# Copying 70 weight chunks inside device memory into contiguous rows before the expert stage

## The reference, cut to what matters

```
pl = modulate(xl, norm1, sh1_l, sc1_l) @ w_in          # 1024 x 6832, the last 4096 columns are gate logits
...                                                    # four mixers on parts of pl: MLA, GQA, mLSTM, Hyena
acc = sum_i sigmoid(gate_i) * (y_i @ w_branch[i])
x = x + g1 * (acc @ w_out)                             # 1024 x 1024
h = modulate(x, norm2, sh2, sc2)
q = h @ peer_wq                                        # 1024 x 2048, eight heads of 256 columns
...                                                    # scores against subkeys, top 16 of 16384 experts per head
out[t] = sum_k share * gelu(peer_u[idx[t,k]] . h[t]) * peer_v[idx[t,k]]
```

## Time and profile before

| | us |
|---|---|
| median of 3 runs | 3304.91 |
| lowest, highest | 3304.67, 3307.84 |
| the profiled execution, its own time | 3291.54 |
| span in its trace | 3289.6 |
| PE busy | 2295.7 |
| DVE busy | 1749.9 |
| POOL busy | 1740.7 |
| ACT busy | 692.3 |
| moved by DMA | 1028.54 MB |

### The profile page before, as it was taken

How to read it: one execution, slowest core, us unless ns; L and a number is a source line. 1 busy time by engine, 2 the same in 40 slices (tenths; PEclk the granted TensorE clock), 3 DMA queues, 4 the chain that set the end, 5 groups by cost and what they waited for, 6 DMA issues and landing times. The chain is left out here.

```text
span 3289.6 us, 32042 instructions
## 1 busy us (share of the span) xinstructions
PE 2295.7 (70%) x10877; PEld 1373.1 (42%) x10877; DVE 1749.9 (53%) x4736; ACT 692.3 (21%) x1336; POOL 1740.7 (53%) x1580
## 2 busy tenths in 40 slices
PE   5999998778957787566777587645799455434435
PEld 2776687644524555232553155321577322101001
DVE  1202335567685556666556745573234766666662
ACT  2235532134111120211102211110442111010000
POOL 0010000467675566777676677776000577777775
PEclk8999999888667898777897588765779767555555
DMA  7677223899999999999999999998302999999997
GB/s 283 209 269 245 64 65 99 293 356 381 323 377 339 354 393 385 350 369 370 374 388 377 342 364 397 398 377 348 115 7 84 311 407 402 404 393 394 405 384 309
DMA packets 395065, 1028.54 MB, mean 313 GB/s; under 512 B 31890, under 2 KB 176282, under 8 KB 393754
## 3 DMA queue, kind: packets, MB, share of 16 engines
q0 software_dynamic: 232064, 847.35, 67.2%
q1 hardware_dynamic: 162794, 179.15, 16.3%
q10 hardware_dynamic: 48, 0.01, 0.0%
HBM read 1019.05 MB, written 7.34 MB: 312 GB/s over the span
## 5 line engine op out<-in xcount | busy, mean ns | idle before, releaser
L1942 POOL DMA_INDIRECT expert_rows<-in_peer_u,chosen x768 | 884.8, 1152 | 840.6 <-DVE chosen L2298 583.2
L2190 DVE CUSTOM_DVE_ANT_0 expert_rows<-expert_rows,h_rows 128x1024 f32<-128x1024 f32 x768 | 937.0, 1223 | 601.0 <-DMA expert_rows<-in_peer_u,chosen 580.8
L2082 PE MATMUL ps<-expert_rows,weights 128*32 128x512 f32 x3072 | 594.0, 855 | 681.3 <-DMA expert_rows<-in_peer_v,row_of 679.3
L1955 POOL DMA_INDIRECT expert_rows<-in_peer_v,row_of x768 | 826.9, 1077 | 403.9 <-PE ps L2082 200.3
L2082 PEld LDWEIGHTS ps<-expert_rows,weights 128*32 128x32 f32 x3072 | 77.2, 125 | 963.5 <-issue 953.0
L1613 PE MATMUL ps<-front,arena 128*128 128x256 f32 x1536 | 384.0, 407 | 76.5 <-DMA arena<-in_w_in 75.7
L1613 PEld LDWEIGHTS ps<-front,arena 128*128 128x128 f32 x1536 | 308.2, 205 | 163.0 <-DMA arena<-in_w_in 59.1
L654 PE MATMUL ps<-front,arena 128*128 128x256 f32 (+1 forms) x816 | 200.0, 403 | 42.6 <-DMA arena<-in_w_in 39.2
L2010 PE MATMUL ps<-h,wq 128*128 128x256 f32 x768 | 200.9, 416 | 2.4 <-ACT h L443 2.4
L654 PEld LDWEIGHTS ps<-front,arena 128*128 128x128 f32 (+1 forms) x816 | 158.6, 198 | 87.9 <-DMA arena<-in_w_in 34.3
L2010 PEld LDWEIGHTS ps<-h,wq 128*128 128x128 f32 x768 | 156.6, 211 | 55.0 <-issue 30.0
(11 more groups left out here) (360 smaller groups left out, 3159.0 us busy)
## 6 DMA issues: line engine op xcount, KB each, us to landing
arena<-in_w_in SPq DMA_DIRECT2D x79, 1024.0 KB, 14.3
arena<-in_ada_w POOLq DMA_DIRECT2D x40, 1024.0 KB, 6.6
wq<-in_peer_wq SPq DMA_DIRECT2D x48, 512.0 KB, 9.4
arena<-in_w_out SPq DMA_DIRECT2D x12, 1024.0 KB, 7.8
expert_rows<-in_peer_u,chosen POOLq DMA_INDIRECT x768, 6.6
expert_rows<-in_peer_v,row_of POOLq DMA_INDIRECT x768, 6.7
ada_w<-in_ada_w SPq DMA_DIRECT2D x4, 2048.0 KB, 23.4
arena<-in_w_branch SPq DMA_DIRECT2D x16, 512.0 KB, 3.4
```

The costliest lines, as they stand in the source:

```text
L1942: nc.gpsimd.indirect_dma_start(x.ring[:, j % self.R, :], None, self.u_rows, bass.IndirectOffsetOnAxis(x.chosen[:, w, q:q + 1], 0)).then_in ...
L1955: nc.gpsimd.indirect_dma_start(x.ring[:, j % self.R, :], None, self.v_rows, bass.IndirectOffsetOnAxis(x.rows[:, w % 4, 4 * c + r:4 * c + r ...
L2082: ins = nc.tensor.matmul(m.ps[to:to + 32, half, :], flat[:, r * P + 32 * c:r * P + 32 * c + 32], x.ring[:, self.place_of["v", a] % self.R, ...
L2190: nc.vector.tensor_tensor_reduce(u, u, x.ht, 1.0, 0.0, ALU.mult, ALU.add, x.dots[:, at:at + 1]).then_inc(self.u_dotted, 1)
```

## The change

A new part, `Relay`, is put into the plan of `opening` behind the two parts that finish the modulation. In it GpSimd issues transfers from memory to memory, with three semaphores in turn, so that a new one is issued when the third before it has landed; its last tick waits for all. Each transfer takes one chunk of weights (runs of 1 KB) and writes it to a tensor of its own in which each of the 128 rows holds all that one partition gets: 8 KB for a chunk of 256 columns of `w_in` or `w_out`, 4 KB for a query chunk. The loads in `experts_beside` then read those tensors. The loads of `opening`, `closing` and `experts` stay as they were. `Projection` packs a chunk's columns without gaps in its ring place.

```diff
+class Relay(Part):
+    FLIGHT = 3
+    def __init__(self, sems, copies):
+        self.copies, self.ticks = copies, len(copies)
+        self.copied = sems(*[f"copied{j}" for j in range(self.FLIGHT)])
+
+    def gpsimd(self, pool, i):
+        to, src = self.copies[i]
+        if i >= self.FLIGHT:
+            pool.wait_ge(self.copied[i % self.FLIGHT], 16 * (i // self.FLIGHT))
+        pool.dma_start(to, src).then_inc(self.copied[i % self.FLIGHT], 16)
+        if i == self.ticks - 1:
+            for j in range(self.FLIGHT):
+                pool.wait_ge(self.copied[j], 16 * len(range(j, self.ticks, self.FLIGHT)))
...
-        sp.dma_start(self.ring[:, c % 2, :, 0:n], self.w_in[:, :, c0:c0 + n]).then_inc(self.ins[c % 2], 16)
+        weights = self.w_in[:, :, c0:c0 + n] if self.flat is None else self.flat[c0, n]
+        sp.dma_start(self.packed(c), weights).then_inc(self.ins[c % 2], 16)
...
-        plan += braid(whole(heads), g[:14], q[54:]) + [(rest0, 0), (rest1, 0)]
+        plan += braid(whole(heads), g[:14], q[54:]) + [(rest0, 0), (rest1, 0)] + whole(Relay(sems, m.copies))
         plan += braid(whole(attn), whole(conv), g[14:22])
...
+        gated = [(O_GATE + 256 * c, 256) for c in range(16)]
+        asked = [(0, 256), (O_GQA, 256), (O_ML, 256), (O_ML + 768, 256), (O_HY, 256), (O_HY + 256, 256), (O_HY + 512, 256)]
+        all_asked = [(0, 256), (256, 160), (O_GQA, 256), (O_GQA + 256, 256), (O_ML, 256), (O_ML + 256, 256), (O_ML + 512, 256),
+                     (O_ML + 768, 272), (O_HY, 256), (O_HY + 256, 256), (O_HY + 512, 256)]
+        for h in range(PH):
+            for c in range(2):
+                flat = nc.dram_tensor(f"flat_q{h}_{c}", (P, KD // 2 * T), F32, kind="Internal").ap()
+                m.flat_q[h, c] = flat.rearrange("p (k n) -> p k n", k=KD // 2)
+                m.copies.append((m.flat_q[h, c], d["peer_wq"][0].rearrange("(k p) n -> p k n", p=P)[
+                    :, 4 * c:4 * c + 4, h * T:(h + 1) * T]))
+        for flats, w, wanted in ((m.flat_in[0], d["w_in"][0], asked + gated), (m.flat_out, d["w_out"][0], [(256 * c, 256) for c in range(4)]),
+                               (m.flat_in[1], d["w_in"][1], all_asked + gated)):
+            for at, n in wanted:
+                flat = nc.dram_tensor(f"flat{NUMBER[1]}", (P, KD * n), F32, kind="Internal").ap()
+                flats[at, n] = flat.rearrange("p (k n) -> p k n", k=KD)
+                m.copies.append((flats[at, n], w.rearrange("(k p) n -> p k n", p=P)[:, :, at:at + n]))
```

More of the change, by code:

```diff
@@ L536, with __init__ @@
 class Projection(Part):
-    def __init__(self, nc, sems, m, w_in, bias, f, kv, s, own, keys, ring, gbias, banks, after, room=(), normed=None, h=None, ahead=False):
-        self.ahead = ahead
+    def __init__(self, nc, sems, m, w_in, bias, f, kv, s, own, keys, ring, gbias, banks, after, room=(), normed=None, h=None, ahead=False, flat=None):
+        self.ahead, self.flat = ahead, flat
         self.h = f.h if h is None else h
@@ L623, in load, with packed @@
         c0, n = self.chunks[c]
-        sp.dma_start(self.ring[:, c % 2, :, 0:n], self.w_in[:, :, c0:c0 + n]).then_inc(self.ins[c % 2], 16)
+        weights = self.w_in[:, :, c0:c0 + n] if self.flat is None else self.flat[c0, n]
+        sp.dma_start(self.packed(c), weights).then_inc(self.ins[c % 2], 16)
+    def packed(self, c):
+        n = self.chunks[c][1]
+        return self.ring[:, c % 2, :, :].rearrange("p k n -> p (k n)")[:, 0:KD * n].rearrange("p (k n) -> p k n", k=KD)
     def sync(self, sp, i):
@@ L649, in tensor @@
         for k in range(KD):
-            w = self.ring[:, c % 2, k, at:at + n]
+            w = self.packed(c)[:, k, at:at + n]
             if i == 0 and self.normed is not None:
@@ L1560, with __init__ @@
     ticks = len(STEPS) + 2
-    def __init__(self, nc, sems, m, w_in, f, ring, sig, banks, after, branches, room=None, flip=0, away=None):
-        self.away = away
+    def __init__(self, nc, sems, m, w_in, f, ring, sig, banks, after, branches, room=None, flip=0, away=None, flat=None):
+        self.away, self.flat = away, flat
         self.room_for, self.flip = room if room else [after, after], flip
@@ L1581, in load @@
         at = O_GATE + 256 * c
-        sp.dma_start(self.ring[:, (c + self.flip) % 2, :, 0:256], self.w[:, :, at:at + 256]).then_inc(self.ins[c % 2], 16)
+        weights = self.w[:, :, at:at + 256] if self.flat is None else self.flat[at, 256]
+        sp.dma_start(self.ring[:, (c + self.flip) % 2, :, 0:256], weights).then_inc(self.ins[c % 2], 16)
     def sync(self, sp, i):
@@ L1735, with __init__ @@
     ticks = KD + 1
-    def __init__(self, nc, sems, m, mod, w_out, acc, ring, lo, banks, after, room):
+    def __init__(self, nc, sems, m, mod, w_out, acc, ring, lo, banks, after, room, flat=None):
+        self.flat = flat
         self.nc, self.m, self.mod, self.acc, self.ring, self.lo, self.banks, self.after = (
@@ L1747, in load @@
             sp.wait_ge(self.mult, 2 * (c - 1))
-        sp.dma_start(self.ring[:, c % 2, :, 0:256], self.w[:, :, c * 256:(c + 1) * 256]).then_inc(self.ins[c % 2], 16)
+        weights = self.w[:, :, c * 256:(c + 1) * 256] if self.flat is None else self.flat[256 * c, 256]
+        sp.dma_start(self.ring[:, c % 2, :, 0:256], weights).then_inc(self.ins[c % 2], 16)
     def sync(self, sp, i):
@@ L1797, with __init__ @@
     R, LV = 10, 20
-    def __init__(self, nc, sems, m, mod, d, l, passes, h, x, banks, after, kept=1):
+    def __init__(self, nc, sems, m, mod, d, l, passes, h, x, banks, after, kept=1, flat=None):
+        self.flat = flat
         self.nc, self.m, self.mod, self.d, self.l, self.passes, self.h, self.x = nc, m, mod, d, l, passes, h, x
@@ L1889, in ask_queries @@
     def ask_queries(self, sp, b, c, head):
-        sp.dma_start(self.x.wq[:, b, c, :, :], self.d["peer_wq"][self.l].rearrange("(k p) n -> p k n", p=P)[
-            :, 4 * c:4 * c + 4, head * T:(head + 1) * T]).then_inc(self.wq_in[2 * b + c], 16)
+        weights = self.d["peer_wq"][self.l].rearrange("(k p) n -> p k n", p=P)[:, 4 * c:4 * c + 4, head * T:(head + 1) * T]
+        if self.flat is not None:
+            weights = self.flat[head, c]
+        sp.dma_start(self.x.wq[:, b, c, :, :], weights).then_inc(self.wq_in[2 * b + c], 16)
     def place(self, v):
@@ L2561, in experts_beside @@
         norm2l = Norm(nc, sems, m, mod, 3 * KD, CTX, h2, m.rs, 7, (), False, True)
-        peer = Peer(nc, sems, m, mod, d, l, [CTX, 0], h2, x, (2, 3), [])
-        proj = Projection(nc, sems, m, d["w_in"][l], bias(l), f, kv, 0, True, False, ring, gbias[:, :], (4, 5), [])
+        peer = Peer(nc, sems, m, mod, d, l, [CTX, 0], h2, x, (2, 3), [], flat=m.flat_q)
+        proj = Projection(nc, sems, m, d["w_in"][l], bias(l), f, kv, 0, True, False, ring, gbias[:, :], (4, 5), [],
+                          flat=m.flat_in[0])
         heads = Heads(nc, sems, m, vec, d, l, f, kv, 0, True, False, heads_memory(arena, Z), (6, 7),
@@ L2571, in experts_beside @@
         gates = Gates(nc, sems, m, d["w_in"][l], f, cut(arena, Z, 2, KD, 256), cut(arena, Z + 4096, 12, T), (4, 5),
-                      conv.done, branch)
+                      conv.done, branch, flat=m.flat_in[0])
         branch.gates = gates
@@ L2575, in experts_beside @@
                         [(branch.acc_done, len(STEPS)), (gates.mult, len(STEPS)), (gates.out, len(STEPS))],
-                        [(gates.mult, len(STEPS))])
+                        [(gates.mult, len(STEPS))], m.flat_out)
         norm2c = Norm(nc, sems, m, mod, 3 * KD, 0, h2, cut(arena, 2048, T), 6,
@@ L2589, in experts_beside @@
         proj_n = Projection(nc, sems, m, d["w_in"][l + 1], bias(l + 1), f, kv, 1, True, True, ring, gbias[:, :], (4, 5),
-                            known, known)
+                            known, known, flat=m.flat_in[1])
         heads_n = Heads(nc, sems, m, vec, d, l + 1, f, kv, 1, True, True, heads_memory(arena, Z), (6, 7), proj_n.done)
         gates_n = Gates(nc, sems, m, d["w_in"][l + 1], f, cut(arena, Z, 2, KD, 256), cut(arena, Z + 4096, 12, T), (4, 5),
-                        heads_n.done, None, away=sigs)
+                        heads_n.done, None, away=sigs, flat=m.flat_in[1])
         conv_n = Hyena(nc, sems, m, vec, d, f, hyena_memory(arena, 0, Z), spectra, (4, 5, 6),
@@ L2638, in build @@
         sigs = nc.dram_tensor("sigs", (P, len(STEPS), T), F32, kind="Internal").ap()
+        gated = [(O_GATE + 256 * c, 256) for c in range(16)]
+        m.flat_out, m.flat_in, m.copies = {}, [{}, {}], []
+        asked = [(0, 256), (O_GQA, 256), (O_ML, 256), (O_ML + 768, 256), (O_HY, 256), (O_HY + 256, 256), (O_HY + 512, 256)]
+        all_asked = [(0, 256), (256, 160), (O_GQA, 256), (O_GQA + 256, 256), (O_ML, 256), (O_ML + 256, 256), (O_ML + 512, 256),
+                     (O_ML + 768, 272), (O_HY, 256), (O_HY + 256, 256), (O_HY + 512, 256)]
+        m.flat_q = {}
+        for h in range(PH):
[7 more added lines that the diff above has]
+            for at, n in wanted:
```

(4 more changed lines are left out.)

## The result

The changed kernel takes 3252.19 us (median of 4 runs, 3247.76 to 3256.75) against 3306.38 us; the ratio is 0.9831, 95% interval [0.9807, 0.9854]: 54 us faster. In a later comparison of more runs it took 3241.52 us against 3303.61, ratio 0.9808 [0.9775, 0.9842]. The forecast had been slower by 72 us; what came is rival A, whose price was 44 us.

What follows compares the result with a forecast made beforehand. Opening bound by TensorE with DMA engines three quarters idle, expert stage bound by DMA; +126 (copy overrun) - 36 (loads) - 18 (waits) = +72 us, so 3364 profiled, 3377 on the median; range 3235 to 3435.

Steps and rivals of the forecast that it cites:

- rival A: Engines from 306 to 569 us: copies overlap read and write, no overrun, 44 us won, about 3261; chance 0.39.
- What bounds the kernel: Opening bound by TensorE with DMA engines three quarters idle; expert stage, 569 to 2295 us, bound by DMA.
- What a copy costs: Copies in the opening at 200 GB/s take 323 us, end at 695 us, 126 us after the old end.
- the low end: Copies in the opening: read and write side by side at the slower's 348 GB/s, 186 us, nothing added.
- the point that decided (258): Copy rate in GB/s at which the opening's overrun equals the expert stage's gain of 54 us.
- the forecast's own range: Whole kernel: 3305 + 105 - 60 = 3350 to 3305 + 175 - 45 = 3435 us.
- GpSimd's issuing: Opening: issuing 70 copies occupies GpSimd 50 to 201 us, inside 263 either way; nothing added.
- The opening's own loads: Opening's weight chunks, sharing engines with copies: 0 to 40 us on the PE path, nothing taken; about 10 if copies fit.
- The loads after it: Expert stage: 73.1 MB go from 1 KB runs to 8 KB (queries 4 KB), 210 to 174 us, 36 saved.
- Waits that go: Expert stage: chunks landing sooner release PE and ring slots sooner; 18 us taken, between 0 and 42.
- the check of the stage: Expert stage: rows at 395 and SP's loads at 348 GB/s give 1628 of 1726 us, explaining it up to 98.
- B: Expert stage: expert rows, not weights, set it, so 36 and 18 fall away; +126, 3431; chance 0.09.

Runs made afterwards that it cites:

- the 1 KB landings: The change with ring rows 272 columns apart, so a partition's 8 KB land in eight 1 KB pieces: 3305.44 us, ratio 1.0020 to the kernel before.

## Why the prediction was wrong

**What bounds the kernel**: right. The opening had its DMA engines three quarters idle, the expert stage is bound by them, and the stage shrank as bytes per microsecond rose.

**What a copy costs**: this step failed, and with it the sign. I took 200 GB/s, by the argument that "a copy passes it twice", reading and writing in turns, and priced 323 us of the engines and an overrun of 126 us. The runs show 347 to 354 GB/s, some 187 us, the low end of 186, and no overrun: the copies are done near 545 us, before 570, the sign that the prediction had named for this step. Reading and writing do not take turns, which by the 419 GB/s of the earlier trace rows would give 209 at most. The argument had nothing in the rows to rest on; that loads and stores each run at 419 GB/s alone (a level, not a bound: single slices of the earlier trace rows stand at 433 to 459) says what a single direction does, not what both do together, and the middle between two guesses of one kind was taken where the ends, 174 and 348, lay on either side of the point that decided (258). The reason given for the low end fell too: long source runs leave the rate where it is. Why it is 350 and not 419 stays open; it hangs on neither the length of the source's runs nor the number in flight (344 with two, while the queue's packets move); rows written other than 4 and 8 KB long were not tried.

The Trainium skill, page "DMA: Bandwidth & Descriptors", section "Latency and other measured facts", has 214 GB/s per direction for copies between memory tensors issued from the sync and scalar queues. This kernel's copies, with GpSimd as the issuer and rows of 4 and 8 KB, ran at 350; the measurement decides. The +105 in the forecast's own range is the overrun by that 214; by the 209 of the rows it would have been +113.

**GpSimd's issuing**: no part of the bound, as said; a copy of 1 MB occupies GpSimd 0.84 us, near the lower of the bounds (0.72 to 2.9).

**The opening's own loads**: nothing in the sum, "about 10 us" in rival A. Measured 18.1 us: a chunk takes 19.2 us to land where doubling gave 10. A share of one half was assumed between the two queues; what the runs show is that a queue with 1 KB packets gets little beside one with 3.8 KB (12.6 us with two copies in flight, 19 with three, 22.7 with six) and less beside 6.1 KB (33 us, three in flight).

**The loads after it**: 36 us by 73.1 MB at 348 and 419 GB/s. SP's queue took 274 us of the engines before and 240 after, 34 less: this term was right in size and reason, and the 1 KB landings confirm it from the other side (265).

**Waits that go**: 18, out of 0 to 42. The stage lost 69; 34 are SP's packets, and 18 are the expert rows' own packets, 1389 us of the engines in place of 1407. That leaves 17 for time in which neither queue's packets moved, so this term came out near its size.

**The other queue's packets**: nothing in the sum, measured 18. Short packets also cost the long ones beside them: in the five profiles whose w_in chunks all move in 1 KB packets, short landings among them, the expert rows' packets take 1404 to 1410 us of the engines, in the others 1388 to 1394. The earlier trace rows had room for it: 81.5% of 1726 us is 1407, where 395 GB/s gives 1359. That is half of the 98 us that the check of the stage left unexplained, and I passed over it.

**Rivals**: A came, at 54 us (62 in the later comparison) where 44 was its price, with 34 + 18 + 17 - 18 = 51 in the profile's stages. That 44 is so near to it is in part luck: the opening's loads cost 8 more than priced, and the expert rows' packets gave 18 that were not priced at all. B is refuted: the stage does shrink. The measured time is inside the range; the chances had A at 0.39 against 0.47 for the forecast.

## What to carry to other kernels

A stage bound by DMA with weights in 1 KB runs can be shortened by rewriting them, in an earlier stage whose DMA engines stand idle, into runs as long as the other queue's packets; here 4 KB was as good as 8 within 9 us of the stage, which itself varies by as much. By this kernel's figure, price the rewrite at about 350 GB/s, each byte counted once, and look for its cost in the loads that share the engines with it, above all short ones, rather than in its own length. Where an unknown rate decides the sign, the place to look is the value at which it does so, and the likeliest value should not be an argument without a row.

## What was not expected of the hardware

- A copy from memory to memory, reading and writing the same memory, moves 347 to 354 GB/s on 16 engines, with source runs of 1 KB and of 8 KB alike, against 348 for a load in 1 KB runs and 419 for one in 8 KB.
- Plain transfers issued by GpSimd with 1 KB source runs appear as packets of 3.8 KB on average, SP's loads with 1 KB pieces as packets of about 1 KB (93.59 MB in 89 864), and the split of the engines between the queues goes with the packets: 1 MB in 1 KB pieces lands in 5.2 us alone, in 17 beside the expert rows' 4 KB, in 19 beside copies in 3.8 KB packets and in 33 beside 6.1 KB on average, three copies in flight each. The number in flight counts too: beside 3.8 KB packets it is 12.6 with two and 22.7 with six.
- The length of the pieces that land counts as much as that of the runs read: contiguous memory read into rows 272 columns apart lands in 17.3 us, as from the scattered matrix.
- The last stage, the same code in all kernels, took 734.8 to 762.4 us from one execution to the next.
